# Three weight strips side by side behind four norms, the third in the norm's own PSUM bank

## The reference

```python
u = rmsnorm(x, norm_mix_w);  proj = u @ w_in + b_in        # norm "mix"
...
u = rmsnorm(x, norm_ffn_w)                                 # norm "ffn0"
up, gate = split(u @ w_ffn_up)
a = causal_dwconv(up, ffn_conv_w, ffn_conv_b)
x = x + (silu(a) * gate) @ w_ffn_down
x = rmsnorm(x, norm_final_w)
...
h = modulate(rms_norm(x, g_ffn1), sh1, sc1)                # norm "ffn1"
x = x + 0.5 * (1 + ga1) * (silu(h @ w1_gate) * (h @ w1_up)) @ w1_down
h = modulate(rms_norm(x, g_mix), sh2, sc2)                 # norm "mix2"
x = x + (1 + ga2) * hybrid_mixer(h)                        # fox_f, sb_q, sb_k, sb_v, ... = split(h @ w_in)
h = modulate(rms_norm(x, g_ffn2), sh3, sc3)                # norm "ffn2"
x = x + 0.5 * (1 + ga3) * (silu(h @ w2_gate) * (h @ w2_up)) @ w2_down
```

## Time and profile before

| | |
|---|---|
| median of three runs | 1873.3 us |
| the profiled execution | 1873.89 us, span 1872.2 us |
| TensorE matmul busy | 98% of the span |
| TensorE weight load busy | 82% |
| VectorE / ScalarE / GpSimd busy | 53% / 36% / 2% |
| mean DMA rate | 107 GB/s |
| mean granted TensorE clock | 0.996 of full speed |

### The profile page before, as it was taken

How to read it: one execution, slowest core, us unless ns; L and a number is a source line. 1 busy time by engine, 2 the same in 40 slices (tenths; PEclk the granted TensorE clock), 3 DMA queues, 4 the chain that set the end, 5 groups by cost and what they waited for, 6 DMA issues and landing times.

```text
span 1872.2 us, 20783 instructions
## 1 busy us (share of the span) xinstructions
PE 1835.6 (98%) x8585; PEld 1526.9 (82%) x8585; DVE 995.6 (53%) x1357; ACT 673.8 (36%) x1008; POOL 38.1 (2%) x73
## 2 busy tenths in 40 slices
PE   6899999999999999999999999999999999999998
PEld 5688888887888888878888888788888778888887
DVE  5555554457777766783433334656767453333332
ACT  5344442234322322342222222464666342232222
POOL 0000000000000000000000000011200000000001
PEclk9999999999999999999999999999999999999999
DMA  3222223254677565333333332321121323333323
GB/s 113 78 79 79 79 79 96 85 155 147 199 223 257 190 202 185 110 87 91 93 98 91 101 96 87 88 57 47 45 68 35 86 79 94 101 92 100 99 87 96
DMA packets 321715, 200.02 MB, mean 107 GB/s; under 512 B 6696, under 2 KB 311126, under 8 KB 321622
## 3 DMA queue, kind: packets, MB, share of 16 engines
q1 hardware_dynamic: 320128, 196.17, 34.9%
q0 software_dynamic: 640, 2.10, 0.4%
q10 hardware_dynamic: 854, 0.43, 0.1%
HBM read 196.57 MB, written 2.10 MB: 106 GB/s over the span
## 4 chain that ended last, share of the span: by engine, by line
PE 93%; DVE 3%; ACT 2%; DMA 0%; issue 0%; SPq 0%; POOL 0%; ACTq 0%; DVEq 0%
PE ps L1349 92%; PE ps L1352 2%; DVE t_b L834 1%; DMA x_in<-in_x 0%; ACT w_hi L376 0%; DVE u_lo L824 0%; DVE u_lo L822 0%; ACT L387 0%; ACT u_hi L403 0%; DVE x L849 0%; DVE u_lo L1217 0%; DVE ssum L812 0%; ACT rstd L389 0%; ACT rstd L390 0%; DVE k_lo L1142 0%
## 5 line engine op out<-in xcount | busy, mean ns | idle before, releaser
L1349 PE MATMUL ps<-u_hi,w_hi 128*128 128x512 f32 x1688 | 667.5, 395 | 8.8 <-DVE u_lo L822 3.3
L1349 PE MATMUL ps<-u_hi,w_lo 128*128 128x512 f32 x1688 | 659.4, 391 | 0.0
L1349 PE MATMUL ps<-u_lo,w_hi 128*128 128x512 f32 x1688 | 659.0, 390 | 0.0
L792 DVE TENSOR_TENSOR w_lo<-w_raw,w_hi 128x1024 fp32r<-128x1024 f32 (+2 forms) x307 | 364.5, 1188 | 271.3 <-ACT w_hi L376 270.5
L376 ACT ACTIVATE w_hi<-w_raw 128x1024 fp32r<-128x1024 f32 (+2 forms) x307 | 314.2, 1024 | 235.8 <-DMA w_raw<-in_w_down 80.0
L1349 PEld LDWEIGHTS ps<-u_hi,w_hi 128*128 128x128 f32 x1688 | 318.3, 189 | 82.2 <-issue 10.8
L1349 PEld LDWEIGHTS ps<-u_hi,w_lo 128*128 128x128 f32 x1688 | 318.0, 188 | 67.4
L1349 PEld LDWEIGHTS ps<-u_lo,w_hi 128*128 128x128 f32 x1688 | 318.4, 189 | 66.3 <-issue 2.4
L1349 PE MATMUL ps<-y_hi,w_hi 128*128 128x512 f32 x656 | 256.0, 390 | 0.0
L1349 PE MATMUL ps<-y_hi,w_lo 128*128 128x512 f32 x656 | 255.4, 389 | 0.0
L1349 PE MATMUL ps<-y_lo,w_hi 128*128 128x512 f32 x656 | 255.2, 389 | 0.0
(11 more groups left out here) (266 smaller groups left out, 1416.8 us busy)
## 6 DMA issues: line engine op xcount, KB each, us to landing
mod_raw<-in_w_mod SPq DMA_DIRECT2D x72, 512.0 KB, 4.8
w_raw<-in_w_in SPq DMA_DIRECT2D x71, 512.0 KB, 3.9
w_raw<-in_w_ffn_up SPq DMA_DIRECT2D x44, 512.0 KB, 4.0
w_raw<-in_w_gate SPq DMA_DIRECT2D x44, 512.0 KB, 3.8
w_raw<-in_w_up SPq DMA_DIRECT2D x44, 512.0 KB, 3.8
w_raw<-in_w_down SPq DMA_DIRECT2D x32, 512.0 KB, 3.9
w_raw<-in_w_ffn_down SPq DMA_DIRECT2D x16, 512.0 KB, 4.1
w_raw<-in_w_down SPq DMA_DIRECT2D x16, 384.0 KB, 3.4
```

The source lines that it names most:

```text
L792: e.tensor_tensor(w_lo[u % SLOTS][:, 0:n_k, :], w_raw[u % SLOTS][:, 0:n_k, :], f32(w_hi[u % SLOTS][:, 0:n_k, :]), ALU.subtract).then_inc(l ...
L1349: return e.matmul(out_, lhsT, rhs, start=start, stop=stop, skip_group_check=skip)
```

## The change

`unit_pair` is replaced by a new `unit_three` behind the norms "ffn0", "ffn1", "ffn2" and "mix2"; the first norm ("mix") keeps its pair. The third unit of the four groups gets bank 7 as its PSUM bank, and its writing waits for `rstd_set`, after which the norm's total in that bank has been read. Which semaphore counts its reading out is unchanged (`bank_read[u % 2]`). The number of instructions on every engine is unchanged.

```diff
         def ubank(u):
+            if u in THIRD:
+                return ps[:, AUX, :]
 
             return ps[:, 3 if u == U["w_o"] + 2 else u % 2, :]
...
+            def unit_three(u0, ready):
+
+                for v in range(u0, u0 + 3):
+                    e.wait_ge(lo_cut, v + 1)
+                    if v in THIRD:
+                        e.wait_ge(rstd_set, SQ[THIRD[v]] + 1)
+                    elif v >= 2:
+                        e.wait_ge(bank_read[v % 2], v // 2)
+                for k in range(KC):
+                    e.wait_ge(ready[0], ready[1] + k + 1)
+                    for v in range(u0, u0 + 3):
+                        c = v % SLOTS
+                        ins = three(ubank(v), (w_hi[c][:, k, :], w_lo[c][:, k, :]), (u_hi[:, k, :], u_lo[:, k, :]), k == 0, k == KC - 1)
+                        if k == KC - 1:
+                            ins.then_inc(unit_done, 1)
...
                     if part == 0:
-                        unit_pair(U[f, "up", 0], u_act, (u_lo_set, FILL[f"ffn{f}"] * KC))
-                    for t in range(2 if part == 0 else 0, 2 * tiles):
+                        unit_three(U[f, "up", 0], (u_lo_set, FILL[f"ffn{f}"] * KC))
+                    for t in range(3 if part == 0 else 0, 2 * tiles):
                         unit(U[f, "up", part] + t, u_act)
...
-            unit_pair(u, u_act, (u_lo_set, FILL["mix2"] * KC))
-            unit(p0 + 1, u_act)
+            unit_three(u, (u_lo_set, FILL["mix2"] * KC))
             e.wait_ge(bank_read[u % 2], u // 2 + 1)
```

More of the change, by code:

```diff
@@ L305, in bank @@
             return ps[:, b, :]
+        THIRD = {U[f, "up", 0] + 2: f"ffn{f}" for f in range(3)} | {U["gate_f"] + 2: "mix2"}
         def ubank(u):
+            if u in THIRD:
+                return ps[:, AUX, :]
             return ps[:, 3 if u == U["w_o"] + 2 else u % 2, :]
```

## The result

The changed kernel takes 1889.91 us (median of six runs, 1887.41 to 1891.96) against 1873.3 us (1871.27 to 1873.73) before. The ratio is 1.0088 with a 95% interval of 1.0075 to 1.0101: 0.9% slower. The profiled execution took 1889.55 us, with a span of 1887.8 us.

A forecast was written before the change was run, and what follows sets the result against it. TensorE, busy 98% of the span, was taken to bound the kernel. Reader chains of 10.1 us plus 5.7 us for the clock made 15.8 us; against the 1873.3 us median, 1889.1 us was forecast, range 1883.0 to 1892.5.

The forecast's parts named there:

- Reader chains: Behind the four norms, fourth strips wait for the first strip's readers and start later: 10.1 us, the 3.3 us gain included.
- the restart: A matmul starting behind a pause follows about 0.08 us later; added at ffn1 and ffn2.
- Loads: SyncE's loads of the fifth to seventh strips start close together: nothing, up to 2 us if they crowd.
- The clock: Half-speed stretches behind the new pauses: 2.3 us at ffn0, 1.7 at mix2, 1.7 at one of ffn1 and ffn2; 5.7 us.
- The rule that was weighed: Only longer gaps lower TensorE's clock: only ffn0 and mix2 would pay, 4.0 us, time 1887.4 us.
- holding clock: Rival: the new pauses do not drop TensorE's clock, or hardly; 1883.4 us, chance 0.15.
- long low stretches: Rival: the clock falls at all four norms and stays low, or loads crowd; up to 1895.0 us, chance 0.15.
- kept ahead: Rival: fourth strips find bank and cut ready, leaving only the gain; 1870.0 us, chance 0.02.

The follow-up runs named there:

- e2: The kernel before with only the third strip's result moved to bank 7, pair first and third strip behind it; 1871.52 us, ratio 0.9987.
- e5: The changed kernel with the feed-forward stages' fourth strip cut right behind the norm and a repeated table load behind mix2 left out; 1876.55 us.
- e3: The kernel before with three strips side by side behind ffn0 alone; 1879.88 us, ratio 1.0035.
- e4: The kernel before with three strips side by side behind mix2 alone; 1876.87 us, ratio 1.0016.
- e7: Against the kernel before: three strips side by side behind ffn1 and ffn2, fourth strip cut early, its result in bank 6; 1870.39 us.
- e1: The changed kernel with dummy matmuls filling the four pauses ahead of the fourth strips; 1881.09 us, against 1889.91 us without them.
- e10: e7 with all four third strips in bank 7 and dummy matmuls in three pauses outside these norms; 1867.58 us, ratio 0.9971 to the kernel before.
- e6: Against the kernel before: three strips side by side behind ffn1 and ffn2 only, fourth strip cut early in all feed-forward stages; 1872.11 us.
- e11: The kernel before with only dummy matmuls (18, 38 and 22) added in its three own pauses; 1870.91 us, ratio 0.9986.

## Why the prediction was right

**Reader chains, 10.1 us.** Right, norm by norm, at the place and with the releaser that were forecast. Forecast were 4.66, 1.41, 2.32 and 1.56 us for the later start of the fourth strip, with 0.08 for the restart at two of them; measured 4.67, 1.41, 2.31 and 1.57. e2 shows that the bank has no part in them, e5 that they follow the work in the chain, e3 and e4 that they add.

**Loads, nothing.** Right. The fifth strip's load is issued at 466.77 behind "ffn0", and no wait for a strip beyond the fourth appears; e7 shows the same with a fourth strip that starts 1 us earlier than before.

**The clock, 5.7 us.** Right in its sum, and e1 shows its cause: with the pauses filled, 5.8 us went away behind the four norms. In its parts it was off: "ffn0" 1.3 instead of 2.3, "mix2" 2.8 instead of 1.7, and of "ffn1" and "ffn2" indeed one, "ffn2", with 1.6 to 1.7. That they added up to the forecast so closely is luck: the six runs spread over 4.6 us, and the mean granted clock goes with them (0.994 in the two runs at 1887.4 and 1887.5 us, 0.991 or 0.992 in the four at 1889.6 to 1892.0), while the chains don't vary from run to run in the profiles (21.72, 21.70 and 21.73 us behind "ffn0" in the changed kernel, e1 and e3).

**The rule that was weighed.** The Trainium skill, "TensorE: Matmul & The Clock Gate", section "Why this matters for your kernels", ties the fall to the longer gaps between bursts. The trace agrees for "ffn0" and "mix2" and disagrees for "ffn2", where a pause of 2.2 us was followed by half speed; e10 shows a second such case. The 3.1 us pause in the `w_o` stage shows the other side. Nine of the kernels have it, and half speed followed it in six of their profiled executions (before, after, e2, e3, e5, e6) and not in three (e1, e4, e7). As a border by length the rule does not hold here. What the forecast set against a holding clock, that every pause of 2.5 us and more in the trace was followed by half speed, was true of that one execution and is no rule either.

**The rivals.** The holding clock did not come by itself, and was made in e1 (1881.1 us, where 1883.4 was the price; the difference lies outside the four pauses, as told at e1). The long low stretches came at one norm of four. The readers never kept ahead.

## What to carry to other kernels

Work that is moved forward to fill one wait may be the cover of another: before strips are put side by side, measure the time from the end of the first result to the release that the next strip needs, and compare it with what is left to issue, here 6.4 us ("ffn0"), 3.6 ("ffn1"), 4.7 ("mix2") and 3.6 ("ffn2") against 1.2. Running strips in step makes all of them end together and so leaves nothing over the first reader; it paid only where the chain was first shortened (early cuts) and cut off from the next strip (a bank of its own). The cheap part of the change, the third bank, was worth more alone than with the rest. How much of e7's gain comes from the step itself was not measured by itself, but e10 has a hint: behind "ffn0" it keeps the pair, with the third strip in bank 7 and the fourth cut early, and there the fourth strip starts 16.59 us after the first product, where running in step reached 16.45 with one bank more.

## What the runs showed of the hardware

A pause of TensorE costs its length and, often, a stretch at half speed behind it: in the changed kernel pauses of 5.1, 2.9 and 2.2 us were followed by some 3.4, 6.4 and 3.4 us at the 1.2 GHz level, which cost 1.3, 2.8 and 1.6 us. The pause of 2.3 us behind "ffn1" was not. The same pause can go either way: the one of 3.1 us in the `w_o` stage was followed by half speed in six of nine profiled executions, the one of 2.5 us ahead of the first product behind norm "mix" in seven of nine (not in e1 and e2), the one of 1.5 us ahead of `k` in none of twelve. So the same program differs by a few microseconds from run to run. Dummy matmuls in the four pauses of the changed kernel gave back 5.8 us and held nothing up (e1). A half-speed stretch ahead of a wait that another engine ends costs nothing: e11's first 18 dummies removed one, and the wait behind it ended 18.06 us after the first product as before.
